# Twelve of the attention gate's projections moved ahead of the recurrence in the filler order of a hybrid decoder step

## The chip, the cores and the metric

The kernel runs on one core of one Trainium2 chip. The metric is the device time of one execution in microseconds (us). TensorE (PE) multiplies matrices into PSUM, VectorE (DVE) and ScalarE (ACT) work lane by lane, GpSimd (POOL) here splits weights and gathers cache rows, and SyncE (SP) issues the other DMAs. Each engine works through its own list of instructions in order, and semaphores hold an instruction back until another engine or a DMA has done its part.

## The reference

One layer of a decoder for 256 prompt tokens and 64 sample tokens (320 token columns together), in float32. The part before the experts is what matters here:

```python
h = _rmsnorm(x, ln1)
xr, gr, q, k, v, qi, ki, wi, gm_r, gm_a = jnp.split(h @ w_in, offs, axis=-1)
...
attn = attend(q, k, v, qi, ki, wi, pos)          # index scores, top-k keys, softmax over them
rnn, conv_new, h_new = _rglru_branch(xr, gr, ...) # width-4 conv, two gates, a linear recurrence
mixed = jax.nn.sigmoid(gm_r) * (rnn @ w_br_rnn) + jax.nn.sigmoid(gm_a) * (attn @ w_br_attn)
x = x + mixed @ w_out
x = x + _hier_moe(_rmsnorm(x, ln2), ...)
```

`attend` for the prompt keeps the top 64 keys of each query, for the sample tokens the top 256 of 1088. The outputs are the two token blocks and the new keys, values, index keys, convolution tails and recurrence states.

## The kernel before

**Units.** The input projection and the branch projections are cut into units of 128 output channels for all 320 tokens. `plan` lists them in order with the weight loads they need: `q`, `k`, `qi`, `ki`, `v`, then for each of the eight chunks of the recurrence `xr` (its input), `gr` (its output gate) and `ga`/`gx` (the recurrence's two sigmoid gates, small block-diagonal products), then `gmr` (16 units of the recurrence's merge gate) with `brr` (16 units of the recurrence branch), `gma` (16 units of the attention's merge gate), `bra` (attention branch) and `out`. A projection unit on PE is 48 products of 320 columns at L1345: 16 blocks of the contraction, three products each, since weights and inputs are split in a high and a low part to keep float32 accuracy. `brr` and `bra` units are eight unsplit float32 blocks at L1332.

**Splitting.** Each 1 MB weight tile lands in one of two raw slots, ACT writes its high part (`high`, L1591, two halves of 128x1024), and DVE the low part (`low`, L1863), or POOL (L1227) for the tiles in `on_pool`, which are those split between the steps `sc` and `sel`. ACT may overwrite a high part only when the unit two tiles back is done. SP issues a load when the slot's previous tile is split.

**Order.** `schedule` writes one list of steps. The attention's own steps stand in a fixed order: `pi`, twelve times `si_t`, `si_s`, `si_w` (index scores), `sc`, `ptk`, then for the eight prompt blocks `pa_l` (logits), `pa_t` (transposed probabilities), `pa_v` (values), with 32 rounds `tk` of the sample's top-k between them, then `sel`, and for the eight sample sequences `sa_t`, `sa_l`, `sa_p`, `sa_v`. `fill_in` puts the units from `xr` 0 to the last `gma` between these steps, one after the other as `plan` lists them, in halves (`half` is the first eight blocks, `unit` the rest); `ga` and `gx` count for nothing. What is left over follows the last step. PE, ACT and POOL go by this list. DVE goes by `vector_order`, the same list in which a unit's evacuation is moved behind the next attention step. Here the stretches are called the index stretch (`pi` 0 up to `pa_l` 0), the prompt stretch (`pa_l` 0 up to `sa_t` 0) and the sample stretch (from there to `bra` 0).

**The recurrence.** A chunk's work is serial over two engines. ACT copies `xr` out of PSUM (L1640), DVE convolves it (L2115 to L2122), PE makes `ga` and `gx` (L1324), ACT applies sigmoid, tanh and exp with table loads (L1654 to L1665), DVE forms the gain (`lru_gain`, L2076 to L2080), ACT takes a root (`lru_root`, L1680), and DVE scans (`lru_scan`, L2088 to L2098). `lru_gain` of a chunk stands behind its `gx`, `lru_root` and `lru_scan` two chunks later, behind `xr`. ACT may write `gx` only when the scan of the chunk before is done. Two PSUM banks serve all units in turn, so a unit waits until the one two places back is evacuated. `brr` waits for all eight scans.

**Spills.** A `gmr` or `gma` unit leaves a sigmoid in a ring of four places (`sgm`, the memory of `qiT`). `brr` multiplies into it. Pairs of finished places go to DRAM through SP (`branch_spill`), which issues the spill of a pair four loads later, once both places are evacuated and the spill before it has landed; ACT waits for it before it reuses the place. All come back in one DMA before `bra` 0 is evacuated.

## Time and profile before

| | |
|---|---|
| median of 3 runs | 2013.89 us (2001.0, 2013.89, 2014.17) |
| profiled execution | 1999.31 us, span 1997.5 us |
| PE busy | 1844.2 us, 92% |
| DVE busy | 1158.2 us, 58% |
| ACT busy | 886.0 us, 44% |
| POOL busy | 118.3 us, 6% |
| mean granted TensorE clock | 0.945 of 2.4 GHz |
| chain that ended last | PE 82%, DVE 12%, ACT 3%, issue 2%, DMA 1% |

The span is first to last instruction of the profiled execution; the execution's own time is 1.8 us above it. Busy means that an instruction of the engine ran, and one engine's idle time matters only where another waits for it. Times in the trace count from the start of the span.

### The profile page before, as it was taken

The numbers are of one execution on the slowest core, as the hardware profiler recorded it, in microseconds if no ns is written. First come the engines' busy times: TensorE is split into PE (matmuls) and PEld (weight loads), VectorE is DVE, ScalarE is ACT, GpSimd is POOL, SyncE is SP. The second block draws the span as 40 slices with busy tenths as digits, with TensorE's granted clock in tenths as the row PEclk, the third lists the DMA queues.
The fourth block names the chain that finished last, engine by engine and source line by source line (L and its number), as shares of the span: only waits on it lengthen the run. The fifth ranks groups of instructions, "written<-read, shape, count | busy, mean of one in ns | idle before, by whom it ended". The sixth has DMA issues, their size and how long they took to land.

```text
span 1997.5 us, 24602 instructions
## 1 busy us (share of the span) xinstructions
PE 1844.2 (92%) x9628; PEld 1535.2 (77%) x9628; DVE 1158.2 (58%) x1381; ACT 886.0 (44%) x987; POOL 118.3 (6%) x75
## 2 busy tenths in 40 slices
PE   5999888658999999999999899999999999997898
PEld 3898768647887777987997688678868877884898
DVE  4885547888842132323442478768846875884532
ACT  3342355354444344311322267647726763773332
POOL 0100005140321000000000000000000000000000
PEclk8999989879999999999997699999979999998899
DMA  7443524232355354673654189959947994995540
GB/s 216 127 127 97 142 64 108 61 90 88 110 150 182 122 167 128 168 257 118 177 143 148 42 281 367 321 173 365 357 157 242 366 349 149 367 357 128 159 120 27
DMA packets 385910, 365.35 MB, mean 183 GB/s; under 512 B 18388, under 2 KB 361476, under 8 KB 383688
## 3 DMA queue, kind: packets, MB, share of 16 engines
q1 hardware_dynamic: 381704, 345.07, 55.0%
q0 software_dynamic: 4096, 18.88, 2.7%
q8 instruction: 62, 1.02, 0.2%
q14 instruction: 48, 0.39, 0.1%
HBM read 353.19 MB, written 10.72 MB: 182 GB/s over the span
## 4 chain that ended last, share of the span: by engine, by line
PE 82%; DVE 12%; ACT 3%; issue 2%; DMA 1%; DVEq 0%; POOL 0%; SPq 0%; ACTq 0%
PE psum L1345 22%; PE psum L635 18%; PE psum L652 8%; PE psum L1332 7%; PE psum L708 6%; PE psum L618 5%; PE psum L670 2%; PE psum L1273 2%; PE psum L1510 2%; PE psum L1532 1%; PE psum L584 1%; PE psum L1507 1%; PE psum L701 1%; DVE weights_low L1863 1%; DVE arena L2007 1%
## 5 line engine op out<-in xcount | busy, mean ns | idle before, releaser
L839 DVE TENSOR_TENSOR weights_low<-arena,weights_high 128x2048 fp32r<-128x2048 f32 x192 | 439.5, 2292 | 89.8 <-ACT weights_high L734 89.8
L1345 PE MATMUL psum<-input_high,weights_high 128*128 128x320 f32 x1264 | 407.6, 322 | 47.1 <-ACT arena L1654 25.5
L734 ACT ACTIVATE weights_high<-arena 128x2048 fp32r<-128x2048 f32 x192 | 367.1, 1915 | 96.4 <-PE psum L635 59.0
L1345 PE MATMUL psum<-input_low,weights_high 128*128 128x320 f32 x1264 | 397.1, 314 | 0.0
L1345 PE MATMUL psum<-input_high,weights_low 128*128 128x320 f32 x1264 | 396.7, 314 | 0.0
L1345 PEld LDWEIGHTS psum<-input_high,weights_high 128*128 128x128 f32 x1264 | 243.9, 193 | 64.3 <-ACT arena L1654 30.8
L1345 PEld LDWEIGHTS psum<-input_low,weights_high 128*128 128x128 f32 x1264 | 244.4, 193 | 1.1
L1345 PEld LDWEIGHTS psum<-input_high,weights_low 128*128 128x128 f32 x1264 | 243.5, 193 | 0.1
L1863 DVE TENSOR_TENSOR weights_low<-arena,weights_high 128x1024 fp32r<-128x1024 f32 x128 | 150.9, 1221 | 112.1 <-ACT weights_high L1591 112.1
L635 PE MATMUL psum<-weights_high,gathered_high 128*128 128x512 f32 x512 | 205.6, 402 | 0.0
L1591 ACT ACTIVATE weights_high<-arena 128x1024 fp32r<-128x1024 f32 x162 | 161.9, 1050 | 92.9 <-PE psum L1345 64.1
L635 PE MATMUL psum<-weights_low,gathered_high 128*128 128x512 f32 x512 | 202.8, 396 | 0.0
L635 PE MATMUL psum<-weights_high,gathered_low 128*128 128x512 f32 x512 | 202.4, 395 | 0.0
L1332 PE MATMUL psum<-arena 128*128 128x320 f32 x512 | 139.8, 433 | 0.0
L1332 PEld LDWEIGHTS psum<-arena 128*128 128x128 f32 x512 | 96.4, 190 | 39.5 <-issue 0.7
L635 PEld LDWEIGHTS psum<-weights_high,gathered_low 128*128 128x128 f32 x512 | 96.8, 189 | 22.9
L635 PEld LDWEIGHTS psum<-weights_high,gathered_high 128*128 128x128 f32 x512 | 96.8, 189 | 22.5 <-issue 0.4
L635 PEld LDWEIGHTS psum<-weights_low,gathered_high 128*128 128x128 f32 x512 | 96.9, 189 | 21.6
L652 PE MATMUL psum<-weights_high,hidden_high 128*128 128x512 f32 x256 | 101.8, 398 | 6.9 <-DVE hidden_low L965 6.9
L652 PE MATMUL psum<-weights_high,hidden_low 128*128 128x512 f32 x256 | 101.3, 396 | 0.0
L652 PE MATMUL psum<-weights_low,hidden_high 128*128 128x512 f32 x256 | 100.8, 394 | 0.0
L1227 POOL TENSOR_TENSOR weights_low<-arena,weights_high 128x1024 fp32r<-128x1024 f32 x34 | 82.8, 2454 | 232.8 <-ACT weights_high L1591 232.7
(315 smaller groups left out, 2410.0 us busy)
## 6 DMA issues: line engine op xcount, KB each, us to landing
arena<-in_w SPq DMA_DIRECT2D x384, 512.0 KB, 6.3
arena<-in_w_in SPq DMA_DIRECT2D x64, 1024.0 KB, 5.6
arena<-in_w_out SPq DMA_DIRECT2D x16, 1024.0 KB, 5.8
arena<-in_w_ple_gate SPq DMA_DIRECT2D x16, 1024.0 KB, 6.1
arena<-in_w_br_rnn SPq DMA_DIRECT2D x8, 1024.0 KB, 5.5
arena<-in_w_br_attn SPq DMA_DIRECT2D x8, 1024.0 KB, 5.3
branch_spill<-arena SPq DMA_DIRECT2D x14, 320.0 KB, 6.8
arena<-branch_spill SPq DMA_DIRECT2D x1, 4480.0 KB, 16.8
```

The source lines that it names most:

```text
L618: last = mm(bank(q)[:, P * a:P * (a + 1)], htok[0:n, tt, P * k:P * (k + 1)], S[0:n, tt, :], start=(tt == 0), stop=(tt == 2))
L635: last = mm(bank(e % 2), x[:, c:c + P], y[:, 512 * k:512 * (k + 1)], start=(q == 0 and k == 0 and n == 0), stop=(q == 3 and k == 3 and n = ...
L652: last = mm(bank(4 + n), x[:, P * k:P * (k + 1)], y[:, 512 * n:512 * (n + 1)], start=(e == 0 and k == 0 and a == 0), stop=(e == EPG - 1 an ...
L670: mm(bank(2 + d % 2, T), outst[:, P * d:P * (d + 1)], ST[:], start=True, stop=True).then_inc(s["sc_mm"], 1)
L708: last = mm(bank(j % 2, T), x[:, P * k:P * (k + 1)], y[:], start=(k == 0 and n == 0), stop=(k == KD - 1 and n == 2))
L734: nc.scalar.activation(stage[m % STG][0][:], mslots[m % MRING], ACT.Identity).then_inc(s["high"], 1)
L839: v.tensor_tensor(lo[:], mslots[m % MRING], hi[:].bitcast(F32), ALU.subtract).then_inc(s["split"], 1)
L1227: nc.gpsimd.tensor_tensor(lo[:, c], raw[:, c], hi[:, c].bitcast(F32), ALU.subtract).then_inc(tile_split, 1)
L1332: last = mm(acc[:, 0:T], w[:, k, :], (rnnT if kind == "brr" else qT)[:, k, :], start=(k == 0), stop=(k == 7))
L1345: last = mm(acc[0:m, 0:T], x[:, P * k:P * k + m], y[:], start=(k == 0 and n == 0), stop=(k == KD - 1 and n == 2))
L1591: nc.scalar.activation(stage[t % 2][0][:, c], slots[n % RING][:, c], ACT.Identity).then_inc(tile_high, 1)
L1863: v.tensor_tensor(lo[:, c], raw[:, c], hi[:, c].bitcast(F32), ALU.subtract).then_inc(tile_split, 1)
```

## The change

`plan` now lists the units `gma` 0 to 11 straight behind `v` and ahead of `xr` 0. `EARLY` is 12, and `GSPILL`, the number of `gma` places that go to DRAM, is the same 12 as before. So `schedule`, whose filler now begins at `gma` 0, puts these twelve into the index stretch and the beginning of the prompt stretch, and `xr`, `gr`, `ga`, `gx`, `gmr` and `brr` move back by twelve units. Only `gma` 12 to 15 are left behind `brr`. The counts with which ACT and SP wait for spills follow the new order of pairs (`nth`), and ACT's first sigmoid into the ring waits for the second `pi`, since the ring is the memory that `pi` reads. Every instruction is still there, in another place. With the tiles' numbers, `on_pool` grows from 17 tiles (26 to 42) to 21 (26 to 46).

```diff
+EARLY = KD - 4
...
     unit("v", 1, [va, vb])
+    for j in range(EARLY):
+        unit("gma", j, [load("w_in", O_GMA + P * j, P)])
     for c in range(CR):
         unit("xr", c, [load("w_in", O_XR + P * c, P)])
...
-    for j in range(KD):
+    for j in range(EARLY, KD):
         unit("gma", j, [load("w_in", O_GMA + P * j, P)])
...
-    first = next(i for i, u in enumerate(units) if u[0] == "xr")
+    first = next(i for i, u in enumerate(units) if u[0] == "gma")
...
-            front = next(n for n in range(len(loads)) if loads[n][1] >= unit_at[("gr", 1)])
+            front = next(n for n in range(len(loads)) if loads[n][1] >= unit_at[("gma", 3)])
...
                     r = (j if kind == "brr" else KD + j) - 1
-                    sp.wait_ge(spill_out, 16 * (r // 2 + 1))
+                    nth = (GSPILL + j if kind == "brr" else j) // 2
+                    sp.wait_ge(spill_out, 16 * (nth + 1))
...
                 elif kind in ("gmr", "gma"):
-                    r = i if kind == "gmr" else KD + i
-                    if r >= 4:
-                        act.wait_ge(spill_out, 16 * (r // 2))
+                    nth = GSPILL + i if kind == "gmr" else i if i < GSPILL else KD + i
+                    if nth >= 4:
+                        act.wait_ge(spill_out, 16 * (nth // 2))
+                    elif nth == 0:
+                        act.wait_ge(pi_mm, 2)
```

What this makes of the order shows in three places. Seven added lines shift line numbers: `high` is L1591 before and L1596 now, DVE's L2028 is L2035 now, and so on.

First, ACT in the index stretch. Before, around `ga` and `gx` of chunk 0:

```order
L1591 ACTIVATE weights_high<-arena 128x1024 x2
L1654 ACT_TABLE_LOAD
L1654 ACTIVATE arena<-psum,arena 128x344
L1661 ACTIVATE arena<-psum,arena 128x344
L1664 ACTIVATE arena<-arena 128x344
L1665 ACT_TABLE_LOAD
L1665 ACTIVATE arena<-arena 128x344
L1716 ACTIVATE arena<-psum 128x512
```

Now, at the same depth of the list:

```order
L1713 ACTIVATE arena<-psum 64x512
L1679 ACTIVATE arena<-psum 128x320
L1723 ACTIVATE arena<-psum 128x512
L1596 ACTIVATE weights_high<-arena 128x1024 x2
L1723 ACTIVATE arena<-psum 128x64
L1712 ACTIVATE arena<-psum 64x512
```

The gates' five activations and table loads are gone from this stretch; a unit leaves one sigmoid (L1679).

Second, DVE in the second half of the prompt stretch, from `pa_l` 5 to `pa_t` 5 before:

```order
L2028 TENSOR_TENSOR arena<-psum,arena 128x1024
L2030 TENSOR_REDUCE arena<-arena 128x4
L2031 TENSOR_SCALAR arena<-arena 128x4
L2005 MAX arena<-arena 64x8
L2007 MATCH_REPLACE arena<-arena 64x1088
L2037 RECIPROCAL arena<-arena 128x4
L2038 TENSOR_TENSOR arena<-arena 128x1024
```

Now, the end of the same stretch between `pa_l` and `pa_t`, behind the top-k round:

```order
L2129 SCALAR_TENSOR_TENSOR arena<-arena 128x344 x3
L2095 TENSOR_TENSOR arena<-arena 128x344
L2096 TENSOR_SCALAR arena<-arena 128x8
L2097 COPY arena<-arena 128x8
L2098 SCALAR_TENSOR_TENSOR arena<-arena 128x344
L2100 COPY arena<-arena 128x1
L2101 COPY arena<-arena 128x8
L2102 TENSOR_TENSOR arena<-arena 128x256
L2105 TENSOR_TENSOR arena<-arena 128x64
L2044 RECIPROCAL arena<-arena 128x4
L2045 TENSOR_TENSOR arena<-arena 128x1024
```

A convolution and a scan stand ahead of the product (L2045) that `pa_t` waits for, where before the product followed the top-k round.

Third, DVE behind `sel`, the end of the sample's top-k. Before, two weight tiles and the first sample logits follow:

```order
L1952 TENSOR_SCALAR arena<-arena 64x1088
L2015 COPY arena<-arena 128x64 x2
L1863 TENSOR_TENSOR weights_low<-arena,weights_high 128x1024 x4
L2052 TENSOR_REDUCE arena<-psum 128x1
```

Now the convolution of chunk 7 and the scan of chunk 5 follow, and behind them the gains and scans of chunks 6 and 7:

```order
L2022 COPY arena<-arena 128x64 x2
L1870 TENSOR_TENSOR weights_low<-arena,weights_high 128x1024 x2
L2122 COPY arena<-arena 128x3
L2123 COPY arena<-arena 128x24
L2127 TENSOR_SCALAR arena<-arena 128x344
L2129 SCALAR_TENSOR_TENSOR arena<-arena 128x344 x3
L2095 TENSOR_TENSOR arena<-arena 128x344
...
L1870 TENSOR_TENSOR weights_low<-arena,weights_high 128x1024 x2
L2083 TENSOR_SCALAR arena<-arena 128x344
L2084 RECIPROCAL arena<-arena 128x344
```

So `ga` 7 and everything behind it on PE come after a chain that begins at the end of `sel`.

## Rows read from the trace of the kernel before

**Rows 1.** Page, part 2: DVE's busy tenths in 40 slices of the span.

```profile
DVE  4885547888842132323442478768846875884532
```

**Rows 2.** Windows of the index, prompt and sample stretches, under their heading's columns.

```profile
195.90:350.50 154.60, 133.90 (x785) 115.24 (x785) 91.45 (x137) 74.30 (x111) 29.15 (x14) 0.90 0.38 103
350.50:565.50 215.00, 168.09 (x953) 143.39 (x953) 181.54 (x267) 94.94 (x167) 60.60 (x27) 0.87 0.33 96
565.50:875.10 309.60, 304.28 (x1818) 256.23 (x1817) 81.57 (x120) 122.62 (x152) 19.69 (x21) 1.00 0.52 163
```

**Rows 3.** Timeline of PE at chunk 0's gates: start, us, instruction, idle before.

```profile
250.45 1.32 PE L1324 MATMUL psum<-arena 128*128 128x344 f32 x4
255.53 0.64 PE L1345 MATMUL psum<-input_high,weights_high 128*128 128x320 f32 x1 [3.75 <-ACT arena L1654]
```

**Rows 4.** Windows of three half units: two behind gates, one without (middle).

```profile
255.50:261.80 6.30, 6.27 (x24) 6.10 (x24) 3.25 (x4) 2.86 (x4) 0.00 (x0) 0.54 0.64 169
263.80:267.60 3.80, 3.80 (x28) 3.61 (x28) 0.69 (x1) 1.12 (x3) 0.00 (x0) 1.00 0.00 0
...
345.20:350.50 5.30, 5.26 (x25) 5.07 (x25) 2.69 (x3) 2.47 (x4) 2.61 (x2) 0.68 0.66 175
```

**Rows 5.** Timeline of PE in the prompt stretch: `pa_t` 1, first block after `gx` 7.

```profile
409.86 0.90 PE L1465 MATMUL psum<-arena 128*128 128x128 f32 x3 [16.76 <-DVE arena L2038]
...
454.89 0.64 PE L1345 MATMUL psum<-input_high,weights_high 128*128 128x320 f32 x1 [7.94 <-ACT arena L1654]
```

**Rows 6.** Timeline of DVE from `pa_t` 1 to `pa_t` 2.

```profile
409.72 1.28 DVE L2005 MAX8 arena<-arena 64x8 f32<-64x1088 f32 x1
...
418.39 0.34 DVE L2076 TENSOR_SCALAR arena<-arena 128x344 f32<-128x344 f32 x1 [3.31 <-issue]
...
422.20 0.42 DVE L2044 COPY arena<-psum 128x256 f32<-128x256 f32 x1
...
429.44 0.17 DVE L2115 COPY arena<-arena 128x3 f32<-128x3 f32 x1
...
431.81 0.51 DVE L2088 TENSOR_TENSOR arena<-arena 128x344 f32<-128x344 f32 x1
432.35 2.20 DVE L2089 TENSOR_SCALAR arena<-arena 128x8 f32<-128x8 f32 x1
...
438.61 0.69 DVE L2038 TENSOR_TENSOR arena<-arena 128x512 f32<-128x512 f32 x1
```

**Rows 7.** Timeline of DVE elsewhere in the index and prompt stretches.

```profile
271.12 0.18 DVE L2089 TENSOR_SCALAR arena<-arena 128x8 f32<-128x8 f32 x1
...
384.85 0.29 DVE L1976 COPY arena<-arena 128x256 f32<-128x256 f32 x1
...
395.74 0.68 DVE L2028 TENSOR_TENSOR arena<-psum,arena 128x512 f32<-128x512 f32 x1
...
451.15 0.52 DVE L2080 TENSOR_TENSOR arena<-arena 128x344 f32<-128x344 f32 x1
...
520.00 1.23 DVE L2028 TENSOR_TENSOR arena<-psum,arena 128x1024 f32<-128x1024 f32 x1
...
556.54 1.34 DVE L1944 TENSOR_SCALAR_CACHE_REDUCE arena<-arena 64x1088 f32<-64x1088 f32 x1
...
567.09 2.35 DVE L1863 TENSOR_TENSOR weights_low<-arena,weights_high 128x1024 fp32r<-128x1024 f32 x2
```

**Rows 8.** Windows of PE alone: eight projection units, then fourteen `bra` units.

```profile
815.25:871.59 56.34, 56.34 (x386) 56.34 (x385) 1.00 0.69 219
...
880.30:940.60 60.30, 60.30 (x225) 42.56 (x224) 1.00 0.43 131
```

**Rows 9.** Page, part 6: DMA issues, KB each, us from issue to landing.

```profile
arena<-in_w_in SPq DMA_DIRECT2D x64, 1024.0 KB, 5.6
...
branch_spill<-arena SPq DMA_DIRECT2D x14, 320.0 KB, 6.8
arena<-branch_spill SPq DMA_DIRECT2D x1, 4480.0 KB, 16.8
```

More of the change, by code:

```diff
@@ L318, in build_program @@
     unit_at = {(k, i): n for n, (k, i, _) in enumerate(units)}
-    n_front = unit_at[("xr", 0)]
     first_bra = unit_at[("bra", 0)]
@@ L332, in build_program @@
     PER = 48
-    GSPILL = KD - 4
+    GSPILL = EARLY
     with ExitStack() as ctx:
```

## The prediction, on record before the changed kernel ran

> **What bounds the kernel now.** I read the windows of the three stretches first. In the sample stretch PE is busy 304.3 of 309.6 us at full clock, so PE's own work sets the time, and DVE, at 81.6 us, is free [rows 2]. In the index stretch PE idles 20.7 of 154.6 us, and in the prompt stretch 46.9 of 215.0 us, where DVE is busy 181.5 us. DVE's digits (fifth to twelfth) say the same [rows 1]. The change lies in all three, and moves DVE's recurrence work between them; the part behind `bra` 0 has the same order as before.
>
> The timelines say why PE idles. In the index stretch the first block behind `ga`/`gx` waits for ACT, which evacuates the gate with table loads: gates at 250.45, next block at 255.53 [rows 3]. There are four such places, 5.1, 5.1, 4.4 and 4.4 us from gate to block. In the prompt stretch `pa_t` waits for DVE's product: 16.8 us at `pa_t` 1 [rows 5]. There DVE does, in order, top-k rounds, a gain, a round, the logits, a round, a convolution, a scan, and only then the product [rows 6].
>
> **Index stretch, units `gma` instead of `xr`, `gr`, `ga`, `gx`.** The number of projection units ahead of `pa_l` 0 is unchanged (twelve and a half), all 48 products long. The four gate places go: 19.0 us. Behind each, a half unit ran slow, at a granted clock of 0.54 to 0.68: 6.3 us for the first and 5.3 for the last, against 3.8 for one without a gate [rows 4]; the four cost 8.1 us together. DVE's convolution of chunk 0 also held the second index step a little, about 1 us. So this stretch loses 28 us. What is added hides: a sigmoid per unit on ACT, which is busy only 74.3 of 154.6 us there [rows 2], and spills on SP, whose pairs land in 6.8 us [rows 9] while a unit between two index steps takes some 11 us. Bounds: 19 us if the clock is slow for another reason, 30 if all waits go.
>
> **Prompt stretch.** Here I add up what ends last from one `pa_t` to the next. A full recurrence period on DVE is the one measured from `pa_t` 1 to 2: 29.5 us, of which 8.7 are two rounds and the wait for ACT's gate chain, 3.8 the gain, 7.2 copy, two rounds and logits, 2.4 the convolution, 6.6 the scan, the rest the product [rows 6]. The scan's small operations took 2.20 us while POOL split a tile, and 0.18 without [rows 7]. PE needs about 21 us in such a period (four half units at 3.52, from eight units in 56.34 us [rows 8], gates, attention, and the wait behind the gates), so DVE sets it.
> - `pa_l` 0 to `pa_t` 0: one logit step and three half units, 11.3 us on PE; DVE has only the convolution of chunk 0.
> - to `pa_t` 1: 5.1 us until `pa_v` 0, copy and round 3.0, the prompt's top-k (`ptk`) from 384.85 to 395.74, 10.9 [rows 7], logits and round 4.2, convolution 2.4, product 0.9: 26.5 us, no gain and no scan.
> - to 2 and to 3: 29.5 each.
> - to 4: a gain but neither convolution nor scan; the key block has doubled, so logits and product take 1.23 us per operation in place of 0.68 [rows 7]: 8.7 + 3.8 + 3.0 + 5.3 + 1.5 = 22.3.
> - to 5: no gain: 5.3 + 3.0 + 5.3 + 2.4 + 6.6 + 1.5 = 24.1.
> - to 6 and to 7: 29.5 and 2.5 for the wider blocks, 32.0 each.
>
> Sum to `pa_t` 7: 207.2 us. Then the chain of my third place in the order. DVE: rounds, wait and gain of chunk 5, 13.1; copy and last maximum 1.7; `sel` 10.6, from 556.54 to 567.09; a tile split 2.4 [rows 7]; convolution 2.4; scan 5 without POOL 2.5: 32.7 us. Only then may ACT write `gx` 6, and gain 6 follows after 3 (a second tile split of 2.4 stands there anyway), takes 3.8, and PE's next block comes 3.2 later, as from gain at 451.15 + 0.52 [rows 7] to 454.89 [rows 5]. So the first block of `gmr` 2 starts 42.7 us after `pa_t` 7, though PE has only some 25 us of work until then: a wait of about 17 us, where the same place had 7.9 [rows 5]. From `pa_l` 0 that is 249.9 us. Before, the corresponding place is the end of the prompt stretch, 215.0 us [rows 2], plus 3 for `sa_t` 0 and a wait. This stretch gains 31.9 us.
>
> **Sample stretch.** Behind that place stood 22 projection units and 8 `brr`; now 18 and 16 stand there. A unit is 7.04 us, a block unit 60.30 / 14 = 4.31 us [rows 8]: minus 28.2 plus 34.5, 6.3 us more. The half unit behind the long wait is slow, 2.5 us by the first of [rows 4] against the middle one. At the end, `gma` 12 may be loaded only when `brr` 13 has left its slot, and `gma` 13 when `brr` 15 has: 5.6 us of landing [rows 9] and some 2.3 until the first half is split (half of the 2.35 on DVE [rows 7] and as much on ACT) against 8.6 and 7.04 us of work, a wait of 1.5. ACT's evacuation of `gma` 12 waits for the pair `brr` 12/13, spilled only behind `gma` 14's load, so the last spill, and with it the 16.8 us return of the ring [rows 9], moves some 5 us nearer to `bra` 0's evacuation; I charge 3 for that, between nothing and 8. Sum: plus 13.3 us.
>
> **Total.** -28 + 31.9 + 13.3 = 17 us slower. Against the profiled execution's own 1999.3 us that is 2016.5. The three runs' median lies 14.6 us above that execution, two runs near 2014 and one at 2001; I add 17 to the median: **2031 us**. If the changed kernel's runs fall on the lower of these levels, it is 2018. About 1%, 20 us, is what can be told from no change.
>
> **Rivals.**
> *The clock.* The prompt stretch ran at 0.87 of the full clock [rows 2], and each wait of PE was followed by a slow half unit [rows 4]. If PE stays slow through the whole stretch, its four half units take 6.3 us each and PE needs about 33 us in a period. Then PE sets the periods: 3.5 more in two of them, 10.7 where I have 22.3, 7 where I have 24.1, 1 in the last two: 27 us more, +44, 2058. Against it: the sum's periods were measured with such slow halves in them. It decides once PE's share in a period falls under what lets it recover. The Trainium skill, "TensorE: Matmul & The Clock Gate", section on the HAM clock gate, says that a slow clock is the default and that activity releases it; so it speaks against a change that spreads waits over eight periods in place of four, and by it the sum would be nearer this rival. The trace agrees in part: 1.2 GHz behind a wait, and full speed again at the next half unit but one, 263.80, where the clock is 1.00 [rows 4].
> *POOL's tiles and scans miss each other.* The order of tiles is new. If the five scans from chunk 0 to 4 run outside POOL's splits, each is 4.1 us shorter [rows 6, 7]: -20, in all -3, 2011. For it: scans 0 and 1 did so in the index stretch. Against it: every scan there is set off by the same ACT sequence (copy of `xr`, root, high part, then POOL) as in the measured period.
> *The ring.* SP waits for the spill before, with loads queued behind. Where units follow back to back, at `gma` 8 to 11 and `gma` 12 to 15, PE's slack on a load is 7.04 less 5.6, and a spill lands in 6.8 us: at most 5.4 us for each of three spills, +16, in all +33, 2047. Against it: the same pairs of loads and spills ran back to back in 815 to 872 with PE never idle [rows 8].
> *The other side.* The recurrence fits into what DVE leaves idle in the prompt stretch, 215.0 - 181.5 = 33.5 us [rows 2], which is more than the five convolutions and two gains added, 5 x 2.4 + 2 x 3.8 = 19.6. Then nothing of the 31.9 is lost but the gates' own 5.6 us, and the sum is -28 + 5.6 and no more than the 6.3 of units, less the 7.9 us wait that is covered: -24, 1990. It decides if the waits for ACT in [rows 6] overlap with rounds. Against it: they stand in order on DVE, and already idle in the measured period.
> *Nothing moves.* The order shows that it does.
>
> **Chances.** Forecast 0.48 (own range +5 to +30 us, 2019 to 2044, two fifths of it above 1%), clock 0.12, POOL 0.17, ring 0.13, other side 0.08, nothing 0.02. Slower by over 1%: 0.19 + 0.12 + 0.13 = 0.44; within 1%: 0.29 + 0.17 + 0.02 = 0.48; faster 0.08. The range reaches from the POOL case on the lower level of the runs, 2001, to just above the ring's, 2050, and leaves out the other side and the clock, 0.20.
>
> **What the profile would show.** The index stretch at 126 to 128 us without idle PE behind gates; `pa_t` 1 to 7 all waiting for DVE's product, also where it did not before (4 to 7); scans with 2.2 us operations; about 17 us of idle PE between `sa_t` 0 and `gmr` 2; the sample stretch without new waits; `bra` 0 at about 892 us in place of 876. I am wrong if `pa_t` 4 to 7 come at PE's pace of 18 to 21 us, if the wait ahead of `gmr` 2 is under 8 us, or if PE idles in the index stretch for loads.

## The result, and the profile after

| | before | after |
|---|---|---|
| median | 2007.45 us (1997.89 to 2014.17, 4 runs) | 2041.66 us (2039.76 to 2045.75, 4 runs) |
| profiled execution, span | 1999.31, 1997.5 us | 2041.49, 2039.7 us |
| PE busy | 1844.2 us, 92% | 1863.2 us, 91% |
| DVE busy | 1158.2 us, 58% | 1149.6 us, 56% |

The ratio is 1.0177, with a 95% interval of 1.0122 to 1.0232: the change makes the kernel slower, by between 1 and 2.3%. The same kernel in a second comparison gave 1.0136 (1.0116 to 1.0155). The levels of the runs, below, explain why the two differ.

The page after shows DVE's tenths, to be laid beside [rows 1]. The work has left slices 5 and 6 (5 and 4 before, 3 and 3 now). Slices 7 to 12 show the same digits as before: DVE isn't fuller there, the stretch has become longer, as the windows show (221.7 us of work in 259.0 us, where it was 181.5 in 215.0).

```profile
DVE  4885337888842131222433478738867873885532
```

The windows of the three stretches answer to [rows 2]. They are the index stretch, then `pa_l` 0 up to the first block behind `gx` 7 (which stands behind `sa_t` 0 now), and the rest up to `bra` 0. So the second row ends at another place of the list than the second of [rows 2]. Columns: window, length, busy us of PE, PEld, DVE, ACT and POOL with their counts, then PE's granted clock, DMA share, GB/s.

```profile
193.50:318.00 124.50, 119.26 (x770) 104.23 (x770) 48.05 (x70) 45.70 (x68) 25.12 (x13) 0.96 0.50 137
318.00:577.00 259.00, 179.27 (x1042) 159.18 (x1041) 221.68 (x316) 127.63 (x218) 83.61 (x38) 0.83 0.32 90
577.00:902.10 325.10, 313.94 (x1745) 255.09 (x1746) 76.22 (x128) 115.31 (x142) 19.53 (x20) 0.98 0.46 144
```

The spans of the two profiled executions differ by 42.2 us. Of these, -2.5 lie ahead of `pi` 0 (`pi` 0 starts between 192.7 and 196.4 us over all profiles, so this is no effect of the change), -30.0 in the index stretch, +41 in the second window (by the forecast's own reckoning of 218 us before), +18.5 in the third, and +15.2 behind `bra` 0, where both kernels hold the same instructions in the same order.

**Index stretch.** PE's idle time falls from 20.7 to 5.2 us. What is left is one wait of 5.23 us for the low half of a tile on DVE, which the kernel before has too; no wait for a load or a spill came in.

**Prompt stretch.** PE's timeline shows a wait for DVE's product (L2045) ahead of each `pa_t` but `pa_t` 4, and behind six of them one for ACT's gate chain (L1659). The last three rows are the two gates of chunk 7 and the first block behind them, to be laid beside the second of [rows 5].

```profile
330.94 0.66 PE L1470 MATMUL psum<-arena 128*128 128x128 f32 x4 [1.50 <-DVE arena L2045]
361.69 1.11 PE L1470 MATMUL psum<-arena 128*128 128x128 f32 x4 [14.60 <-DVE arena L2045]
...
391.22 1.12 PE L1470 MATMUL psum<-arena 128*128 128x128 f32 x4 [6.68 <-DVE arena L2045]
396.77 0.63 PE L1350 MATMUL psum<-input_high,weights_high 128*128 128x320 f32 x1 [2.14 <-ACT arena L1659]
...
535.89 1.97 PE L1470 MATMUL psum<-arena 128*128 128x128 f32 x8 [7.19 <-DVE arena L2045]
...
565.87 1.26 PE L1329 MATMUL psum<-arena 128*128 128x344 f32 x2 [4.20 <-ACT arena L1659]
567.48 1.51 PE L1329 MATMUL psum<-arena 128*128 128x344 f32 x2 [0.35 <-ACT arena L1666]
576.96 0.64 PE L1350 MATMUL psum<-input_high,weights_high 128*128 128x320 f32 x1 [7.96 <-ACT arena L1659]
```

From `pa_l` 0 the `pa_t` follow at 13.0, 30.8, 29.5, 29.8, 23.0, 26.3, 32.6 and 33.1 us (forecast 11.3, 26.5, 29.5, 29.5, 22.3, 24.1, 32.0, 32.0), and the block at 576.96 another 41.1 later (forecast 42.7). DVE's timeline tells why the first two are longer. The convolution of chunk 0 meets a split on POOL, whose own row follows; that of chunk 7 meets none.

```profile
324.02 6.05 DVE L2129 SCALAR_TENSOR_TENSOR arena<-arena 128x344 f32<-128x344 f32 x3
...
562.50 1.80 DVE L2129 SCALAR_TENSOR_TENSOR arena<-arena 128x344 f32<-128x344 f32 x3
```

```profile
324.07 5.02 POOL L1232 TENSOR_TENSOR weights_low<-arena,weights_high 128x1024 fp32r<-128x1024 f32 x2 [3.32 <-ACT weights_high L1596]
```

**Sample stretch.** A wait that the forecast didn't have stands at its end, at `brr` 15 on PE, and a second one at `gma` 13:

```profile
863.50 6.06 PE L1337 MATMUL psum<-arena 128*128 128x320 f32 x16 [5.82 <-DVE arena L2146]
...
879.30 0.42 PE L1350 MATMUL psum<-input_high,weights_high 128*128 128x320 f32 x1 [2.71 <-DVE arena L2146]
```

DVE, in its own order, has the low half of `gma` 12's tile (L1870) ahead of the evacuations of `brr` 13 and 14 (L2146); ACT has the tile's high half, which waited for the load:

```profile
860.69 2.36 DVE L1870 TENSOR_TENSOR weights_low<-arena,weights_high 128x1024 fp32r<-128x1024 f32 x2 [11.09 <-ACT weights_high L1596]
862.97 0.88 DVE L2146 TENSOR_TENSOR arena<-psum,arena 128x320 f32<-128x320 f32 x2
```

```profile
859.60 2.00 ACT L1596 ACTIVATE weights_high<-arena 128x1024 fp32r<-128x1024 f32 x2 [14.36 <-DMA arena<-in_w_in]
```

`gma` 12's load, issued at 853.41, needs the slot that `brr` 13 leaves: `brr` 12 starts at 844.61, and two units of 4.36 us later `brr` 13 is done. PE goes on with `brr` 14 in the other bank. But the finished `brr` 13 stays in its PSUM bank until a tile has landed and been split that could not be requested before `brr` 13 was done, and `brr` 15 finds no bank. (The expectation of the kernel with the evacuation first, below, calls this unit `brr` 14.)

**Behind `bra` 0.** The experts come in four groups, each opened by 96 products of 128x128 (L618) that gather the group's tokens. Grouped rows of PE, before, in the stretch ahead of the second group (1280 to 1320.5) and ahead of the third (1450 to 1503.8); busy us, mean ns, idle before:

```profile
L618 PE MATMUL psum<-arena 128*128 128x128 f32 (+1 forms) x96 | 17.0, 308 | 0.0
...
L618 PE MATMUL psum<-arena 128*128 128x128 f32 (+1 forms) x96 | 30.0, 473 | 0.0
```

PE's windows of the two places in the same kernel, columns as above:

```profile
1300.00:1320.00 20.00, 18.47 (x106) 14.02 (x105) 8.97 (x14) 1.79 (x3) 0.00 (x0) 1.00 0.32 105
...
1470.00:1490.00 20.00, 18.53 (x65) 13.84 (x63) 8.06 (x13) 1.20 (x2) 0.00 (x0) 0.57 0.31 105
```

The waits of PE in front of the two are the same, 1.4, 1.5 and 1.7 us, yet one set of these products runs at a granted clock of 1.00 and the other near 0.5 (0.57 in the window above, 0.50 from 1490 to 1504, where PE is busy all the time). It costs 13 us, and with the first expert products about 14. Before, two of the four groups began slowly (1122.4 us behind `bra` 0); after, three did (1137.6). The Trainium skill, "TensorE: Matmul & The Clock Gate", section "What's actually happening", says that the monitor's window runs free of the kernel and that the same kernel can come out differently from run to run. No run here can show the first. The second agrees: the same order of instructions took 1137.6 us behind `bra` 0 in one profile and 1150.8 in the next. In twelve further profiles the part behind `bra` 0 took 1122.1 to 1122.4, 1137.5 to 1138.9, or 1150.4 to 1150.8 us, always with two, three and four slow groups. The runs of the kernel before stand on such steps, 1996 to 2002 and 2011 to 2019 us, with two at 2004.6; the changed kernel's stand at 2040 to 2046, and one at 2057. Compared at three slow groups each, the change costs about 28 us, 1.4%; from `pi` 0 to `bra` 0 the two profiles give 679.1 and 708.6, which is 29.5.

### The profile page after: what moved, and what is told of

It reads as the page before. It is cut to its first block, busy times and chain, and to the rows that moved or that the text cites. A ratio compares the mean times of both kernels' runs of the same rounds, so it can differ in the third digit from the quotient of the medians.

```text
span 2039.7 us, 24606 instructions
## 1 busy us (share of the span) xinstructions
PE 1863.2 (91%) x9628; PEld 1549.5 (76%) x9628; DVE 1149.6 (56%) x1373; ACT 882.9 (43%) x985; POOL 137.1 (7%) x83
## 4 chain that ended last, share of the span: by engine, by line
PE 79%; DVE 13%; ACT 3%; issue 2%; DMA 2%; DVEq 0%; POOL 0%; SPq 0%; ACTq 0%
PE psum L1350 20%; PE psum L639 18%; PE psum L656 8%; PE psum L1337 6%; PE psum L712 6%; PE psum L622 5%; PE psum L674 2%; PE psum L1515 2%; PE psum L1278 2%; PE psum L1537 1%; DVE arena L2129 1%; PE psum L588 1%; DVE weights_low L1870 1%; PE psum L1512 1%; PE psum L705 1%
## 5 line engine op out<-in xcount | busy, mean ns | idle before, releaser
L1350 PEld LDWEIGHTS psum<-input_high,weights_high 128*128 128x128 f32 x1264 | 243.2, 192 | 63.9 <-ACT arena L1659 29.5
L1870 DVE TENSOR_TENSOR weights_low<-arena,weights_high 128x1024 fp32r<-128x1024 f32 x120 | 141.5, 1221 | 124.3 <-ACT weights_high L1596 124.3
L1596 ACT ACTIVATE weights_high<-arena 128x1024 fp32r<-128x1024 f32 x162 | 161.8, 1050 | 113.8 <-PE psum L1350 64.0
L639 PEld LDWEIGHTS psum<-weights_low,gathered_high 128*128 128x128 f32 x512 | 97.6, 191 | 21.8
L1232 POOL TENSOR_TENSOR weights_low<-arena,weights_high 128x1024 fp32r<-128x1024 f32 x42 | 99.8, 2394 | 204.0 <-ACT weights_high L1596 203.9
L622 PE MATMUL psum<-arena 128*128 128x128 f32 (+1 forms) x384 | 107.1, 432 | 0.0
```

Source lines behind the costliest of these rows:

```text
L622: last = mm(bank(q)[:, P * a:P * (a + 1)], htok[0:n, tt, P * k:P * (k + 1)], S[0:n, tt, :], start=(tt == 0), stop=(tt == 2))
L639: last = mm(bank(e % 2), x[:, c:c + P], y[:, 512 * k:512 * (k + 1)], start=(q == 0 and k == 0 and n == 0), stop=(q == 3 and k == 3 and n = ...
L1232: nc.gpsimd.tensor_tensor(lo[:, c], raw[:, c], hi[:, c].bitcast(F32), ALU.subtract).then_inc(tile_split, 1)
L1350: last = mm(acc[0:m, 0:T], x[:, P * k:P * k + m], y[:], start=(k == 0 and n == 0), stop=(k == KD - 1 and n == 2))
L1596: nc.scalar.activation(stage[t % 2][0][:, c], slots[n % RING][:, c], ACT.Identity).then_inc(tile_high, 1)
L1870: v.tensor_tensor(lo[:, c], raw[:, c], hi[:, c].bitcast(F32), ALU.subtract).then_inc(tile_split, 1)
```

## The experiments

All compare with the kernel before, in rounds on the same chip; its median lay between 2011.35 and 2013.88 us in these comparisons, and each ratio is taken within its own. This table holds the stretches of each profile in us, the second one only where its end is the same place.

| kernel | `pi` 0 to `pa_l` 0 | to block behind `gx` 7 | `pi` 0 to `bra` 0 | behind `bra` 0 | median | ratio (95%) |
|---|---|---|---|---|---|---|
| before | 154.4 | | 679.1 | 1122.4 | 2012.8 | 1 |
| after | 124.4 | 259.0 | 708.6 | 1137.6 | 2041.66 | 1.0177 (1.0122-1.0232) |
| after, again | 124.5 | 258.6 | 708.4 | 1150.8 | 2041.43 | 1.0136 (1.0116-1.0155) |
| after, gates apart | 124.6 | | 709.1 | 1137.5 | 2040.5 | 1.0129 (1.0110-1.0148) |
| before, gates apart | 135.3 | | 663.4 | 1122.4 | 1988.54 | 0.9882 (0.9841-0.9923) |
| after, evacuation first | 124.5 | 258.8 | 697.8 | 1138.0 | 2030.99 | 1.0077 (1.0041-1.0113) |
| after, half of POOL's tiles | 124.5 | 263.6 | 715.2 | 1137.6 | 2051.67 | 1.0217 (1.0153-1.0281) |
| after, 16 of 32 rounds | 124.3 | 246.2 | 695.7 | 1150.4 | 2033.78 | 1.0109 (1.0026-1.0193) |
| before, 16 of 32 rounds | 152.3 | | 673.9 | 1138.9 | 2005.83 | 0.9951 (0.9909-0.9993) |
| before, apart and evacuation | 135.1 | | 663.0 | 1122.1 | 1980.87 | 0.9871 (0.9803-0.9939) |
| after, 8 rounds early | 124.4 | 260.0 | 709.4 | 1150.5 | 2045.6 | 1.0173 (1.0127-1.0218) |
| before, apart, evac., 8 early | 142.4 | | 669.7 | 1122.1 | 1999.59 | 0.9926 (0.9895-0.9958) |
| only four `gma` first | 142.9 | | 681.9 | 1137.9 | 2016.31 | 1.0033 (0.9996-1.0070) |
| after, one round moved | 124.6 | 246.6 | 696.3 | 1150.7 | 2029.77 | 1.0097 (1.0062-1.0131) |

**The same kernel again.**

> The changed kernel once more. In its first profile the part behind bra 0 took 1136.7 us against 1121.5 before, although the instructions are the same, and three of the four expert groups began at a slow clock against two before. If that is chance, the number of groups that begin slow differs from run to run, and the time moves in steps of about 14 us: some runs near 2027, others near 2041. If the change causes it, all runs stay at 2038 to 2046 and the profile has three slow groups again.

The stretches repeat to 0.4 us. This profile fell on four slow groups (2056.6 us), so the number of them does vary for one kernel; the other four runs stand at 2040.8 to 2042.5, and none came near 2027.

**The gates' two products apart.** `ga` goes behind the next `xr` and `gx` behind the next `gr`, so a unit of PE's work covers ACT's work on each:

```diff
-        unit("gr", c, [load("w_in", O_GR + P * c, P)])
         if c:
             unit("ga", c - 1, [])
+        unit("gr", c, [load("w_in", O_GR + P * c, P)])
+        if c:
             unit("gx", c - 1, [])
```

(and `gx` 7 behind `gmr` 2.) In the kernel after:

> The changed kernel, with ga and gx of a chunk no longer side by side: ga stands behind xr, gx behind gr, so that each PSUM bank has a whole unit's time to be evacuated and ACT's gate chain runs under PE's products. Theory (the DVE chain sets the prompt stretch, and its wait for ACT's gates is in it): each of five periods with a gain loses the 3.3 us wait, and the 12.5 us of PE waits ahead of gmr 2 shrink by 5 to 8: 20 to 25 us faster than the changed kernel, about 2018. Rival (PE's own work and slow clock set the periods): only the gate holes of 2 to 3 us and the slow halves go, 8 holes of 2.5 and 2 us each, 36 us faster, 2005. Rival (the order of gates does not matter, top-k and scans do): under 8 us.

In the kernel before:

> The kernel before with the same regrouping of gates and nothing else. The four gate places of the index stretch cost 19.0 us and 8.1 us of slow half units; with a unit between ga and gx both should go except the gates' own 5.6 us: 20 us there, and in the prompt stretch three waits of 3.3 us on DVE and most of the 7.9 us hole: 35 us faster than before in all, near 1972. If ACT is late anyway (an extra table load per chunk, since gelu now stands between two sigmoids), 10 us or less.

In the kernel before, the index stretch loses 19.1 us without the change under study, as its window shows against the first of [rows 2]:

```profile
196.00:331.30 135.30, 126.70 (x786) 108.52 (x786) 91.16 (x136) 77.02 (x112) 26.46 (x14) 0.95 0.42 113
```

So about two thirds of what the change gained there come from ACT's gate chain alone, and are to be had in another way. The other half of the expectation failed: from `pa_l` 0 to `bra` 0 the kernel takes 528.1 us in place of 524.7, where some 15 less were expected. PE no longer waits for DVE's product there but a unit earlier, for ACT to copy `xr` out of its bank (L1645). In ACT's list that copy stands behind the exponentials of the same prompt block, for whose logits ACT had waited 19.47 us on DVE:

```profile
382.79 0.63 PE L1347 MATMUL psum<-input_high,weights_high 128*128 128x320 f32 x1 [18.93 <-ACT arena L1645]
```

The changed kernel gains nothing, where 20 to 25 us were expected: its `pa_t` 2 and 3 come 28.7 us after the one before, in place of 29.5 and 29.8, and `pa_t` 7 comes 1.7 us earlier, but from `sa_t` 0 to `bra` 0 PE idles 30.3 us in place of 23.7. It was the place of PE's waits that moved.

**The evacuation ahead of the split.** DVE's order puts a held `brr` evacuation ahead of the next split:

```diff
+        elif what == "split" and held and units[held[0][1]][0] == "brr":
+            out += held + [(what, i)]
+            held = []
```

> The changed kernel with one rule of DVE's order changed: a brr unit's evacuation is not held back behind the split of the next weight tile. In the changed kernel PE idled 5.8 and 2.7 us at brr 14 and gma 13, where DVE had first to split a tile whose load could only start when that very brr unit had finished, and two units behind ran slow (3.9 and 5.3 us for 2.3 and 3.7). Theory: the first wait goes whole, the second shrinks to the load's own lateness of 1 to 2 us: 7 to 10 us faster than the changed kernel. Rival (the load alone is what is late): under 3 us, and PE waits as long for the split of gma 12.

The wait of 5.82 us at `brr` 15 is gone, and one of 1.15 is left, now at `gma` 12:

```profile
862.33 0.41 PE L1353 MATMUL psum<-input_high,weights_high 128*128 128x320 f32 x1 [1.15 <-DVE arena L2149]
```

`bra` 0 comes 10.8 us earlier counted from `pi` 0, and the median falls by 10. The mechanism of the tail is shown.

**Every second of POOL's tiles on DVE**, from tile 31:

```diff
-    on_pool = {t for what, i in pool_steps if what == "split" for t in split_before[i]}
+    on_pool = {t for what, i in pool_steps if what == "split" for t in split_before[i] if t % 2 == 0 or t < 31}
```

> The changed kernel, with every second tile from 31 on split by DVE instead of POOL (eight of the 21): those whose POOL split ran while DVE did a convolution or a scan. In the changed kernel the first two convolutions took 6.05 and 5.84 us for 1.80, and five scans have two operations of 2.2 us for 0.17. Theory (DVE is held by POOL's split): these return to 1.8 and 0.2 us, DVE takes 2.4 us for each tile instead of 4.1 us of waiting, and may wait up to 1 us more for ACT's high part: about 1 us per period, 5 to 12 us faster than the changed kernel. Rival (these operations are slow for a reason of their own): they stay slow, and eight splits of 2.4 us come on top, 15 to 19 us slower.

Neither number came; the kernel is 10 us slower. The operations in question did shrink, and that shows what held them: the two convolutions take 1.80 us and the scans' small operations 0.17. But the split that DVE took over stands on the same path, with a wait for its high half in front. In the period to `pa_t` 3:

```profile
410.96 2.36 DVE L1871 TENSOR_TENSOR weights_low<-arena,weights_high 128x1024 fp32r<-128x1024 f32 x2 [2.45 <-issue]
...
416.13 0.17 DVE L2097 TENSOR_SCALAR arena<-arena 128x8 f32<-128x8 f32 x1
416.34 0.17 DVE L2098 COPY arena<-arena 128x8 f32<-128x8 f32 x1
```

2.45 + 2.36 us are paid for 4.1 saved. In the period to `pa_t` 4 there is no scan and nothing to save, and the split costs 3.7 us, the largest single loss:

```profile
441.98 2.36 DVE L1871 TENSOR_TENSOR weights_low<-arena,weights_high 128x1024 fp32r<-128x1024 f32 x2 [2.33 <-issue]
```

The two periods with the slow convolutions got shorter, by 1.3 and 1.2 us. So the contention is real, and giving every second tile to its other party is no way out of it. Whether the two tiles beside the convolutions alone would pay wasn't tried.

**Half of the sample's top-k rounds left out.** Of the 32 rounds `tk` the odd ones return without work, in both kernels, so the sample's keys are others. The changed one has two runs only.

> The changed kernel without every second round of the sample's top-k (16 of 32 rounds of 2.6 us left out, so the sample's key selection is another). Theory (DVE's chain sets each period): to pa_t 1 5 us less, each of the periods with a gain 2.6 less (the other round lay under the wait for ACT), the others until PE's 21 us: 20 to 27 us faster than the changed kernel. Rival (PE's work at its granted clock sets the periods): under 8 us.

> The kernel before without every second round of the sample's top-k (16 of 32 left out). Theory: only its first four periods are DVE's, so 8 to 13 us faster than before, and the distance to the changed kernel without these rounds falls from 28 us, at equal numbers of slow expert groups, to 10 to 17. Rival (the distance comes from elsewhere): both get faster by the same, the distance stays near 28.

The first part of the changed kernel is 12.9 us shorter and that of the kernel before 5.2, so the distance falls from 29.5 to 21.8. The 12.9 and the 21.8 lie between the numbers of the theory and of its rival, the 5.2 under the theory's 8 to 13. But 16 rounds of 2.65 us are 42 us of DVE's work. Less than a third of it came back, and the next kernels were to find out why.

**The two edits together on the kernel before.**

> The kernel before with ga and gx apart and the brr evacuations ahead of the next split. The gates alone gave 16 to 24 us. In the kernel before no brr unit waited for an evacuation, so the second edit should add nothing, 0 to 2 us: about 1983 with two slow expert groups and 1997 with three. If the held evacuations cost something there too, 5 us more.

At 1980.87 us (0.9871, 0.9803 to 0.9939) it is the fastest kernel of the study. The evacuation's edit adds nothing measurable here (663.0 against 663.4), since in this order the place has no such wait.

**Rounds ahead of the prompt stretch.** DVE waits for 24.22 us ahead of the first logits there. So eight rounds and the prompt's top-k go in front, and none is left behind `pa_l`:

```diff
     steps.append(("sc", 0))
-    for part in range(3):
-        steps.append(("ptk", part))
-    fill_in(10)
...
+    for part in range(6):
+        steps.append(("ptk", part))
+    top(8)
+    fill_in(10)
     for m in range(8):
         steps.append(("pa_l", m))
-        top(1)
...
-        if m == 0:
-            steps += [("ptk", 3), ("ptk", 4), ("ptk", 5)]
```

> The changed kernel with its order of units as it is, but the preparation of the search for the largest scores (ptk 3 to 5) and 8 of its 32 rounds are put ahead of the prompt stretch, where DVE in the changed kernel is idle for 24.2 us before pa_l 0; one round less stands behind each of the eight pa_l. Theory (DVE's chain sets the pace of the prompt stretch): the stretch from pa_l 0 to the first block of gmr 2 gives back what DVE no longer does in it, 8 rounds of about 2.6 us and the preparation, some 24 us (15 to 30), so 259 becomes about 235; the index stretch stays at 124 to 126, and the time is about 2017 (2011 to 2026). Rival (PE's waits there come from the length of a gate chunk's own chain ACT, DVE, POOL and from the split the two engines fight over, not from how much DVE has to do): less than 8 us, 2033 to 2042.

> The kernel before with the gates' two products apart (ga ahead of the next gr, gx behind it), the evacuation of brr ahead of the next split, and the same 8 rounds and ptk 3 to 5 ahead of the prompt stretch, two rounds to each fill of two halves. Theory (DVE's chain): the kernel with the first two edits alone took 1980.9; its PE is idle for 51.6 us in the prompt stretch. 10 to 20 us of that go, so 1961 to 1971 with two expert groups that begin slowly, 1975 to 1985 with three; the index stretch may grow by up to 5 us where a round stands before a split. Rival (in this order PE's waits there are not DVE's load): within 5 us of 1980.9.

The theory fell in both: in the changed kernel the stretch takes 260.0 us. Two things show on DVE. The hole was overfilled: eight rounds took 21.6 us and `ptk` 14.4 (10.9 before, its scan 2.70 us beside POOL's splits in place of 0.69), 36 us for 24, and the first logits are handled at 330.14 in place of 318.73. So `pa_t` 0 came 10.5 us later, and `pa_t` 1, rid of `ptk`, made up 8.9. And in the later periods the round behind `pa_l` had cost next to nothing. Where it was, DVE now waits for ACT:

```profile
408.59 0.17 DVE L2036 TENSOR_SCALAR arena<-arena 128x4 f32<-128x4 f32 x1
410.97 0.17 DVE L2120 COPY arena<-arena 128x3 f32<-128x3 f32 x1 [2.21 <-ACT arena L1646]
```

The periods to `pa_t` 2 and 3 are 28.7 and 29.2 us (29.5 and 29.8 with the round). On the kernel before it was a loss of 6.7 us to `bra` 0 against the kernel with the two edits alone (669.7 and 663.0). There the rounds stand between the fillers of the index stretch, which grew by 7.3 us, with a wait of 4.62 us on PE for ACT at `gx`; the rest gave back 0.6. That the `ptk` alone would fit into the hole is open; it wasn't tried.

**A smaller dose:** only `gma` 0 to 3 first.

```diff
-EARLY = KD - 4
+EARLY = 4
-    GSPILL = EARLY
+    GSPILL = KD - 4
```

(and the counts of spills to match.)

> A smaller dose of the change: only projections gma 0 to 3 come first, gma 4 to 15 stay at the end, and the ring of spills is numbered to match. One chunk's gates (3) now fall behind pa_l 0 that stood before it, where the change puts four (0 to 3) there. Theory (each chunk that goes from the index stretch to the prompt stretch takes its waits out of the one and puts a chunk's gates and convolution on DVE's chain in the other): a quarter of each sum, index stretch about 147 instead of 154.4 (124.4 in the change), prompt stretch about +10, in all +5 to +10 on the kernel before, about 2020 (2013 to 2025). Rival (all of the loss is in the first four or the last four of the moved projections, by the ring or by the tail's loads): then the time stands at one end, 2013 or under, or 2035 and over.

The loss isn't in proportion. The index stretch gains 11.5 us and the rest up to `bra` 0 loses 14.4, in all 2.8; with twelve it is 30.0 against 59.5. The place behind `gx` 7 stands at 491.57 here, ahead of `pa_t` 5, and its wait is 7.31 us, as before (7.94). PE's idle time from `sa_t` 0 on is 2.3 us, against 23.7 in the change. So the first four moved projections trade about evenly. Of the 26.7 us between the two kernels at `bra` 0, 21.4 are PE's idle time from `sa_t` 0 on: what costs is to push the last chunks behind `sel`, where a chain of `sel`, convolution, scan and gain stands bare, and to leave so few `gma` that they follow `brr` at the tail. At which number between 4 and 12 this begins wasn't measured.

**One round moved, DVE's work the same.** After the rounds kernel I looked at one period of the changed kernel as a loop, from one `pa_t` to the next, on DVE:

```profile
395.18 1.27 DVE L2014 MATCH_REPLACE8 arena<-arena 64x1088 f32<-64x1088 f32 x1
399.75 0.34 DVE L2083 TENSOR_SCALAR arena<-arena 128x344 f32<-128x344 f32 x1 [3.30 <-issue]
...
403.76 0.42 DVE L2051 COPY arena<-psum 128x256 f32<-128x256 f32 x1 [0.23 <-PE psum L1481]
404.14 1.29 DVE L2012 MAX8 arena<-arena 64x8 f32<-64x1088 f32 x1
...
406.84 0.69 DVE L2035 TENSOR_TENSOR arena<-psum,arena 128x512 f32<-128x512 f32 x1
...
413.98 2.22 DVE L2096 TENSOR_SCALAR arena<-arena 128x8 f32<-128x8 f32 x1
...
420.26 0.69 DVE L2045 TENSOR_TENSOR arena<-arena 128x512 f32<-128x512 f32 x1
```

Behind the two rounds that follow `pa_t`, DVE still waits 3.30 us for the gates' chain (PE's `ga`, then ACT). The round at 404.14, behind `pa_v`, stands ahead of logits that are already there. So it goes into the wait:

```diff
         steps.append(("pa_t", m))
-        top(2)
+        top(3)
         fill_in()
         steps.append(("pa_v", m))
-        top(1)
```

> The changed kernel, with one of the four rounds of the search in each period of the prompt stretch moved: three stand behind pa_t and none behind pa_v, where two and one stood. DVE's work is the same, to the instruction. Theory, formed after the kernel with 8 rounds ahead of the stretch gained nothing (a period there is a loop through PE, ACT and DVE, and a round costs nothing where DVE would wait for ACT anyway: behind pa_t, where 3.3 to 4.6 us of waiting for the gates' chain are left, and behind pa_l, where the round hid a wait of 2.2 us; only the one behind pa_v lies on the loop): the waits of 3.3, 3.3, 3.3, 3.0, 4.6 and 4.6 us on DVE behind pa_t 1 to 6 shrink by a round's 2.65 us each, the periods of 29.5 us become about 27, and the first block of gmr 2 comes 13 to 18 us earlier (259 becomes 241 to 246), 2023 to 2029 us. Rival (DVE's load sets the stretch, and the two kernels without rounds there lost their gain elsewhere): within 3 us of the changed kernel, 2038 to 2046.

The wait is down to 0.60 us, and the products of `pa_t` 2 and 3 come 26.9 and 27.5 us after the last one:

```profile
400.16 0.34 DVE L2082 TENSOR_SCALAR arena<-arena 128x344 f32<-128x344 f32 x1 [0.60 <-DVE arena L2013]
...
418.38 0.69 DVE L2044 TENSOR_TENSOR arena<-arena 128x512 f32<-128x512 f32 x1
```

The stretch takes 246.6 us (-12.4) and the time falls by 12, just short of the 13 to 18 expected; from `pi` 0 to `bra` 0 it is as much as half of all rounds left out gave (696.3 and 695.7). Of a period's four rounds in the changed kernel, only the one behind `pa_v` lay on the path. The two behind `pa_t` end before the gates' chain does, and so does the third when it is put there; the one behind `pa_l` hid a wait of 2.21 us. The odd rounds left out above were one behind `pa_t` and the one behind `pa_v` in each period, which is why 16 of them gave back no more than this move. It follows that the prompt stretch is set by the loop through PE, ACT and DVE, and not by the sum of DVE's work.

## Why the prediction was right, and where not

It said about +17 us, by a loss in the prompt stretch greater than the gain in the index stretch. The sign and the main mechanism held. The three terms together came to +29.5, at the upper end of the forecast's own +5 to +30; of the 12 us that it was too low, 9.1 are in the prompt stretch.

- **Index stretch, -28:** -30.0. The four waits for ACT's gate chain and the slow halves behind them went, the upper bound of the forecast. No wait for a ring place or a load came in.
- **Prompt stretch, +31.9:** +41. The convolutions' price is the term that was mis-sized: I took 2.4 us from one outside POOL's splits. Chunks 0 and 1 met a split, 6.05 and 5.84 us for the three operations that take 1.80, and this is 1.7 and 4.3 of the 9.1 us missing. I had written of contention only for the scan. The Trainium skill, "SBUF — State Buffer", section "SBUF: two separate sides", says that DVE and GpSimd share a pair of ports under an exclusive lock, for an operation with two SBUF inputs too (against a GpSimd one that reads SBUF), and that the later one blocks; the rows agree: the operations stretch to the length of POOL's split (5.02 us) and past it. Another 2.2 came at `pa_t` 5, where PE waited 1.5 us for POOL's split and DVE 2.98 for PE, and 2.7 in the other periods; the last chain gave back 1.6. The two periods that I took whole from the trace, 29.5, came out at 29.5 and 29.8. `pa_t` 4 didn't wait for DVE's product, against what I had written of `pa_t` 1 to 7.
- **"So DVE sets it":** right as a sum, wrong as a reason. I added up DVE's work and its waits as one list, and the total was the period. But DVE is one part of a loop, with 3.0 us or more of waiting left in each period from `pa_t` 1 on and with rounds that only fill its waits, as the kernels with fewer, earlier and moved rounds show.
- **Wait ahead of `gmr` 2, about 17 us:** the chain from `pa_t` 7 was 41.1 us long, forecast 42.7, and PE's work beside it 25.4, forecast 25. So PE idled 15.7 us, but not in one place: 3.20 behind `gx` 5, 4.55 at the last gates and 7.96 behind them. Between `sa_t` 0 and `gmr` 2, where I had put all 17, it was 12.5. The single wait of 7.96 is no longer than the 7.94 before, and by the letter it is under the 8 us that I had named as a sign of being wrong; the sum of the waits bears the forecast out.
- **Sample stretch, +13.3:** +18.5. "The sample stretch without new waits" failed. The units' 6.3 and the slow half hold, but I charged 1.5 for a late load and 3 for the ring's return. PE's waits for the evacuations were 8.5 us, with a slow unit behind each place, because DVE's order held the evacuation behind the split; with the evacuation first 1.15 are left, which is what the late load itself costs. The ring's return made PE wait for nothing.
- **Rivals.** The clock: no. PE's share of full clock was 0.83 against 0.87, and yet PE waited for DVE in the periods, so there was room for the slow halves. PE did run slow behind its waits for the gates (a granted clock of 0.68 in 367.2 to 372.5, 0.55 in 396.8 to 402.9), and not behind the two of 1.5 us at `pa_t` 0 and 4 (1.00 in 331.3 to 335.0 and in 446.4 to 450.1). That was in the sum. The Trainium skill, "TensorE: Matmul & The Clock Gate", section "What's actually happening", has the rule that the forecast named, a slow clock as the default and activity releasing it; these rows agree, but it didn't decide the time. POOL's tiles and scans missing each other: the reverse happened, more operations met. The ring: no waits. The other side, that waits and rounds overlap: it didn't happen in this order; the moved round shows that a part of it, 12 us, was to be had.
- **The experts.** What I added to the median was the sum alone, on the levels of the runs. The first comparison's 34 us between medians hold 28 of the change; the rest is that the kernel before has runs on its lower level and the changed one showed none in nine. Whether the change makes a slow beginning likelier, or chance did, isn't settled: of seven runs with the evacuation first, two stand 11 us lower, at 2019.5.

## What to carry to other kernels

When work is moved to fill a bound stretch, ask for each piece whether it lies on the loop from one wait to the next or in a wait of its own engine; an engine busy 86% of a stretch (221.7 of 259.0 us) had three of four rounds nearly for free, and then it is their place that counts, not their sum. Look for the waits that the moved work leaves (here ACT's gate chain) before moving it: covering them where they are, by setting `ga` and `gx` apart, gained 1.2%, where moving everything away lost 1.4%. In an in-order engine, don't queue the evacuation that frees a PSUM bank behind a split whose tile can be requested only when that same unit is done.

## What the runs showed of the hardware

- The same instructions behind the same waits of 1.4 to 1.7 us ran at a clock near 0.5 or at 1.00: 30.0 or 17.0 us for 96 products of 128x128. A stage with four such places gives a program whose runs stand on steps of about 14 us, whatever was changed ahead of it. Read a difference of that size only from stretches of the trace.
- Three SCALAR_TENSOR_TENSOR of 128x344 on DVE took 1.80 us alone and 6.05 beside a split on POOL, and an operation on 128x8 took 0.17 us alone and 2.2 beside one. A maximum search over 64x1088 (MAX8) took 1.28 us alone and 1.29 beside one. A scan of 128x256 in the kernel with early rounds took 2.70 in place of 0.69.
